# Gate and up as seven block products in place of eight, with the multiplication of activation and up rows left on GpSimd

## The reference

```python
def conv_ffn(h, prev, w_gate, w_up, conv_w, conv_b, w_down):
    g = h @ w_gate
    u = h @ w_up
    l = g.shape[1]
    gp = jnp.concatenate([prev.astype(g.dtype), g], axis=1)
    gc = conv_b
    for i in range(CONV_W):
        gc = gc + conv_w[i] * gp[:, i:i + l]
    y = (jax.nn.gelu(gc) * u) @ w_down
    return y, gp[:, -(CONV_W - 1):]
```

## Time and profile before

| | |
|---|---|
| median of 3 runs | 1596.8 us (1596.42 to 1599.4) |
| profiled execution, device time | 1597.14 us |
| its span in the trace | 1595.6 us |
| mean granted TensorE clock | 0.996 |
| TensorE busy | 1571.7 us (99%) |
| VectorE busy | 783.5 us (49%) |
| ScalarE busy | 565.6 us (35%) |
| GpSimd busy | 387.9 us (24%) |

### The profile page before, as it was taken

How to read it: one execution, slowest core, us unless ns; L and a number is a source line. 1 busy time by engine, 2 the same in 40 slices (tenths; PEclk the granted TensorE clock), 3 DMA queues, 4 the chain that set the end, 5 groups by cost and what they waited for, 6 DMA issues and landing times.

```text
span 1595.6 us, 27497 instructions
## 1 busy us (share of the span) xinstructions
PE 1571.7 (99%) x10810; PEld 1497.5 (94%) x10810; DVE 783.5 (49%) x1022; ACT 565.6 (35%) x888; POOL 387.9 (24%) x421
## 2 busy tenths in 40 slices
PE   9999989999999999999999999999999999999998
PEld 6899879999999999999988997799999999999997
DVE  3324786665543245553322248857554522555522
ACT  4332266245552123322222323643455411333312
POOL 3370020432221012222306402115222200221223
PEclk9999999999999999999999999999999999999998
DMA  5321253222322223322233213612233232232222
GB/s 199 123 76 54 93 186 140 77 99 96 129 97 92 86 90 109 105 67 77 71 102 123 86 47 135 231 59 72 94 130 105 86 102 89 94 129 79 65 73 92
DMA packets 44415, 161.99 MB, mean 102 GB/s; under 512 B 5793, under 2 KB 8257, under 8 KB 43265
## 3 DMA queue, kind: packets, MB, share of 16 engines
q1 hardware_dynamic: 39680, 129.70, 25.0%
q0 software_dynamic: 2464, 28.26, 4.4%
q10 hardware_dynamic: 2208, 3.15, 0.5%
HBM read 149.08 MB, written 30.88 MB: 113 GB/s over the span
## 4 chain that ended last, share of the span: by engine, by line
PE 89%; DVE 6%; ACT 2%; issue 2%; POOL 1%; POOLq 0%; DVEq 0%; ACTq 0%
PE PSUM L1490 62%; PE PSUM L1540 13%; PE PSUM L1565 6%; PE PSUM L1466 4%; PE PSUM L1780 1%; DVE RS L987 1%; PE PSUM L1718 1%; PE PSUM L1556 0%; PE PSUM L1713 0%; DVE SM L1195 0%; ACT WH L728 0%; ACT PS L799 0%; POOL YT L691 0%; DVE XNL L1357 0%; DVE CT L1392 0%
## 5 line engine op out<-in xcount | busy, mean ns | idle before, releaser
L982 DVE TENSOR_TENSOR WL<-RAW,WH 128x1024 fp32r<-128x1024 f32 (+1 forms) x216 | 294.4, 1364 | 489.1 <-ACT WH L728 488.6
L728 ACT ACTIVATE WH<-RAW 128x1024 fp32r<-128x1024 f32 (+1 forms) x216 | 211.9, 982 | 553.9 <-PE PSUM L1490 385.9
L1490 PE MATMUL PSUM<-XFH,WH 128*128 128x320 f32 x1056 | 240.9, 310 | 1.8 <-DVE WL L982 1.2
L1490 PE MATMUL PSUM<-XFH,WL 128*128 128x320 f32 x1056 | 240.0, 309 | 0.0
L1490 PE MATMUL PSUM<-XFL,WH 128*128 128x320 f32 x1056 | 240.0, 309 | 0.0
L1490 PE MATMUL PSUM<-XNH,WH 128*128 128x320 f32 x864 | 198.2, 310 | 1.0 <-DVE XNL L1357 1.0
L1490 PE MATMUL PSUM<-XNL,WH 128*128 128x320 f32 x864 | 196.8, 309 | 0.0
L1490 PE MATMUL PSUM<-XNH,WL 128*128 128x320 f32 x864 | 196.7, 309 | 0.0
L1490 PEld LDWEIGHTS PSUM<-XFH,WH 128*128 128x128 f32 x1056 | 176.2, 188 | 3.0 <-issue 2.7
L1490 PEld LDWEIGHTS PSUM<-XFL,WH 128*128 128x128 f32 x1056 | 176.3, 188 | 0.0
L1490 PEld LDWEIGHTS PSUM<-XFH,WL 128*128 128x128 f32 x1056 | 176.2, 188 | 0.0
(11 more groups left out here) (230 smaller groups left out, 2341.5 us busy)
## 6 DMA issues: line engine op xcount, KB each, us to landing
RAW<-w_gu SPq DMA_DIRECT2D x88, 512.0 KB, 3.5
RAW<-w_in SPq DMA_DIRECT2D x40, 512.0 KB, 3.6
RAW<-w_down SPq DMA_DIRECT2D x32, 384.0 KB, 3.0
RAW<-w_down SPq DMA_DIRECT2D x32, 320.0 KB, 2.7
CAK<-ca_kt SPq DMA_DIRECT2D x16, 512.0 KB, 4.6
CAV<-ca_v SPq DMA_DIRECT2D x16, 512.0 KB, 5.1
RAW<-w_out SPq DMA_DIRECT2D x16, 512.0 KB, 3.6
ca_kt_copy<-ca_kt POOLq DMA_DIRECT2D x16, 512.0 KB, 4.9
```

The costliest lines, as they stand in the source:

```text
L728: nc.scalar.activation(WH[:, s, 0:width], RAW[:, s, 0:width], ACT.Copy).then_inc(hi_ready[s], 1)
L982: nc.vector.tensor_tensor(WL[:, s, 0:width], RAW[:, s, 0:width], WH[:, s, 0:width].bitcast(F32), ALU.subtract).then_inc(lo_ready[s], 1)
L1490: last = nc.tensor.matmul(PSUM[:, b + a, 0:HALF], w[:, s, P * k:P * (k + 1)], x[:, HALF * a:HALF * (a + 1)], start=start and k == 0 and w ...
```

## The change

From tile 3 (PLAIN) on, gate and up of a tile are taken as one product of 2 x 2 blocks. The rows are up (a11, a12) and gate (a21, a22), the inner blocks are the first and the last four of the eight tiles of D_MODEL, and the columns are the two halves of the frames (b11, b12, b21, b22). Seven products of sums of blocks give all four results, in place of eight: a11 b11, s2 t2, s1 t1, s3 t3, a12 b21, a22 t4, s4 b22. Each has 4 x 3 matmuls of 320 columns and a PSUM bank of its own.

- Frames are scaled by gain and RS ahead of the product (`scale_frames`, into XN), and t1 to t4 are formed; all seven are rounded and get a remainder, once a layer, while tiles 0 to 2 run in the old way.
- For each tile, VectorE forms s1 to s4 (512 columns), ScalarE rounds the seven blocks, VectorE takes the seven remainders. WH and WL hold four of them, EXH and EXL three. Loads alternate between RAW and RAW2.
- ScalarE copies a11 b11 into RS, which is free for it now; VectorE adds the products up (`take_...`) into RS, U3, GP and UT.
- Convolution, gelu, YH and YL of a tile move into the next tile's turn on VectorE and ScalarE. Loops over tiles are written out.
- GpSimd's program is the same: it multiplies UT and CT as before.

The diff, cut to its core:

```diff
+PLAIN = 3
+DOWN_UNIT = FFN_UNIT + 2 * PLAIN
+UNITS = DOWN_UNIT + 2 * KT * FFN_HALVES
 SLOT_USES = UNITS // 2
+QUARTER = KT // 2 * P
+PRODUCTS = ("a11", "s2", "s1", "s3", "a12", "a22", "s4")
+MOVING = {"a11": "b11", "s2": "t2", "s1": "t1", "s3": "t3", "a12": "b21", "a22": "t4", "s4": "b22"}
+BLOCK_SUMS = ("s1", "s2", "s3", "s4")
+FRAME_STEPS = tuple(range(KT)) + ("t1", "t3", "t2", "t4")
+FRAME_PARTS = ("b11", "t1", "t2", "t3", "b21", "t4", "b22")
...
+                def block_round(t, name):
+
+                    if name[0] == "a":
+                        act.wait_ge(quarters_loaded[t % 2], quarters_count(l, t))
+                    else:
+                        act.wait_ge(sum_done, sum_count(l, t, name))
+                    if t in (PLAIN, FF_HALF) and PRODUCTS.index(name) < 4:
+                        n = (FFN_UNIT, PLAIN - 1) if t == PLAIN else (DOWN_UNIT, KT - 1)
+                        product_wait(act, l, n[0] + PRODUCTS.index(name) // 2, n[1])
+                    elif folded_index(l, t):
+                        act.wait_ge(block_used, block_count(l, t, name) - len(PRODUCTS))
+                    nc.scalar.activation(block_slot(name)[0], block_source(t, name), ACT.Copy).then_inc(block_hi, 1)
...
+                def y_round(t):
+                    if t == FF_HALF:
+                        product_wait(act, l, DOWN_UNIT + 1, KT - 1)
+                    act.wait_ge(product_done, CREDIT + 2 * (l * FF_TILES + t) + 2)
+                    nc.scalar.activation(YH[:, t % FF_HALF, :], YT[:, :], ACT.Copy).then_inc(y_hi, 1)
...
+                def take_first(t):
+
+                    act.wait_ge(block_used, block_count(l, t, "a11"))
+                    act.wait_ge(folded, 4 * folded_index(l, t))
+                    if t == PLAIN:
+                        act.wait_ge(up_copied, CREDIT + l * FF_TILES + t)
+                    nc.scalar.activation(RS[:, 0:HALF], block_bank("a11"), ACT.Copy).then_inc(first_taken, 1)
...
-                        nc.scalar.activation(YH[:, f, :], YT[:, :], ACT.Copy).then_inc(y_hi, 1)
+                    for t in range(FF_HALF if h else PLAIN + 1, FF_HALF * (h + 1)):
+                        last, inner = t == FF_HALF * (h + 1) - 1, t != FF_HALF
+                        block_round(t, "s4")
+                        take_first(t)
+                        if not last:
+                            block_round(t + 1, "a11")
+                        if inner:
+                            gelu(t - 1)
+                        if last:
+                            down_round(0, h, 0)
+                        else:
+                            block_round(t + 1, "s2")
+                        if inner:
+                            y_round(t - 1)
+                        if last:
+                            down_round(1, h, 0)
+                        else:
+                            block_round(t + 1, "s1")
+                            block_round(t + 1, "s3")
+                        if not last:
+                            block_round(t + 1, "a12")
+                            block_round(t + 1, "a22")
+                        tap(t)
+                    gelu(FF_HALF * (h + 1) - 1)
+                    y_round(FF_HALF * (h + 1) - 1)
...
+                def block_sum(t, name):
+
+                    a = {"s1": ("a21", "a22", ALU.add), "s2": ("s1", "a11", ALU.subtract),
+                         "s3": ("a11", "a21", ALU.subtract), "s4": ("a12", "s2", ALU.subtract)}[name]
+                    dve.wait_ge(quarters_loaded[t % 2], quarters_count(l, t))
+                    if name in ("s2", "s4"):
+                        dve.wait_ge(sum_done, sum_count(l, t, name) - (1 if name == "s2" else 2))
+                    used = {"s1": (t - 1, "s3"), "s2": (t - 1, "s4"), "s3": (t, "s1"), "s4": (t, "s2")}[name]
+                    if folded_index(l, used[0]) >= 0 and used[0] >= PLAIN:
+                        dve.wait_ge(block_lo, block_count(l, *used))
+                    nc.vector.tensor_tensor(block_source(t, name), block_source(t, a[0]), block_source(t, a[1]), a[2])\
+                        .then_inc(sum_done, 1)
+
+                def block_rest(t, name):
+
+                    dve.wait_ge(block_hi, block_count(l, t, name))
+                    high, low = block_slot(name)
+                    nc.vector.tensor_tensor(low, block_source(t, name), high.bitcast(F32), ALU.subtract)\
+                        .then_inc(block_lo, 1)
...
+                def scale_frames(k):
+
+                    nc.vector.scalar_tensor_tensor(out=XN[:, k, :], in0=X[:, k, :],
+                                                   scalar=GAIN[:, bass.ds(l, 1), 1, k], in1=RS[:, :],
+                                                   op0=ALU.mult, op1=ALU.mult).then_inc(frame_step, 1)
...
+                def take_second(t):
+
+                    i = folded_index(l, t)
+                    dve.wait_ge(block_used, block_count(l, t, "s2"))
+                    dve.wait_ge(first_taken, i + 1)
+                    dve.wait_ge(up_copied, CREDIT + l * FF_TILES + t)
+                    nc.vector.tensor_tensor(RS[:, HALF:], block_bank("s2"), RS[:, 0:HALF], ALU.add).then_inc(folded, 1)
+
+                def take_third(t):
+
+                    i = folded_index(l, t)
+                    dve.wait_ge(block_used, block_count(l, t, "s3"))
+                    dve.wait_ge(gate_copied, CREDIT + 2 * (l * FF_TILES + t))
+                    dve.wait_ge(folded, 4 * i + 1)
+                    nc.vector.tensor_tensor(U3[:, :], block_bank("s3"), RS[:, HALF:], ALU.add).then_inc(folded, 1)
+
+                def take_gate_second(t):
+
+                    gate_free(t)
+                    dve.wait_ge(folded, 4 * folded_index(l, t) + 2)
+                    nc.vector.tensor_tensor(streams[:, 1, :, 2:], streams_of(block_bank("s1")[:, 0:HALF_SAMPLE]),
+                                            streams_of(U3[:, 0:HALF_SAMPLE]), ALU.add)
+                    nc.vector.tensor_tensor(GP[:, 2 + HALF_PROMPT:CONV_ROW], block_bank("s1")[:, HALF_SAMPLE:],
+                                            U3[:, HALF_SAMPLE:], ALU.add).then_inc(gate_copied, 1)
+                    nc.vector.tensor_tensor(RS[:, HALF:], block_bank("s1"), RS[:, HALF:], ALU.add).then_inc(folded, 1)
+
+                def take_up_first(t):
+
+                    dve.wait_ge(block_used, block_count(l, t, "a12"))
+                    dve.wait_ge(product_done, CREDIT + 2 * (l * FF_TILES + t))
+                    nc.vector.tensor_tensor(UT[:, 0:HALF], block_bank("a12"), RS[:, 0:HALF], ALU.add).then_inc(folded, 1)
+
+                def take_gate_first(t):
+
+                    dve.wait_ge(block_used, block_count(l, t, "a22"))
+                    nc.vector.tensor_tensor(streams[:, 0, :, 2:], streams_of(block_bank("a22")[:, HALF_PROMPT:]),
+                                            streams_of(U3[:, HALF_PROMPT:]), ALU.add)
+                    nc.vector.tensor_tensor(GP[:, 2:2 + HALF_PROMPT], block_bank("a22")[:, 0:HALF_PROMPT],
+                                            U3[:, 0:HALF_PROMPT], ALU.add).then_inc(gate_copied, 1)
+
+                def take_up_second(t):
+
+                    dve.wait_ge(block_used, block_count(l, t, "s4"))
+                    dve.wait_ge(folded, 4 * folded_index(l, t) + 3)
+                    nc.vector.tensor_tensor(UT[:, HALF:], block_bank("s4"), RS[:, HALF:], ALU.add)\
+                        .then_inc(up_copied, 1)
...
+                rstd_ready.wait(dve, l, "ffn")
+                dve.wait_ge(pads_zeroed, l + 1)
+                lo(l, FFN_UNIT + 2, 0)
+                take_gate(0)
+                for k in range(4):
+                    scale_frames(k)
+                convolve(0)
+                for k in range(4, KT):
+                    scale_frames(k)
+                take_up(0)
+                lo(l, FFN_UNIT + 3, 0)
+                frame_sum("t1")
+                y_rest(0)
+                frame_rest("b11")
+                lo(l, FFN_UNIT + 2, 1)
...
+                    for t in range(FF_HALF if h else PLAIN + 1, FF_HALF * (h + 1)):
+                        last, inner = t == FF_HALF * (h + 1) - 1, t != FF_HALF
+                        if inner:
+                            take_up_second(t - 1)
+                            convolve(t - 1)
+                        block_rest(t, "s4")
+                        if not last:
+                            block_sum(t + 1, "s1")
+                            block_sum(t + 1, "s2")
+                        take_second(t)
+                        if last:
+                            down_rest(0, h, 0)
+                        else:
+                            block_rest(t + 1, "a11")
+                            block_rest(t + 1, "s2")
+                            block_rest(t + 1, "s1")
+                            block_sum(t + 1, "s3")
+                        take_third(t)
+                        take_gate_second(t)
+                        if inner:
```

(72 more changed lines are left out.)

293 lines of the change are left out of this document (221 added, 72 removed).

## The result

| | before | after |
|---|---|---|
| median of 4 runs each, the same chip | 1597.13 us (1596.42 to 1599.40) | 1616.49 us (1616.32 to 1616.73) |
| span of the profiled execution | 1595.6 us | 1614.7 us |
| mean granted TensorE clock | 0.996 | 0.986 |

The changed kernel takes 1.012 times as long (95% interval 1.0108 to 1.0132): 19.4 us more. The forecast was +36 us, 1633 in a range of 1590 to 1662. The sign, the range and the mechanism held; the size was 17 us too large.

The account below looks back on a forecast made before the run. TensorE's matmuls bound the kernel before; VectorE would bind after, at 14.4 us a folded tile against 12.32. Halves at +17.0 and +1.0 us, over two layers, add 36 to 1597.1: 1633 us, range 1590 to 1662.

Parts of the forecast that it names:

- The tile: Steady folded tile: VectorE needs 14.4 us, against TensorE's 12.32 and 14.08 before the change.
- back-to-back work: VectorE's 23 instructions over 9,824 columns in a folded tile, one behind the other: 12.0 us.
- waits for the direct neighbour: Four times in a folded tile a VectorE instruction waits for the one right ahead: 0.22 us each, together 0.9.
- GpSimd's multiplication holds a sum: In each folded tile GpSimd's multiplication falls on VectorE's sums for the next tile and holds them up: 0.9 us.
- convolution waits for the tap: In each folded tile convolution on VectorE waits for ScalarE's tap after the last copy into GP: 0.2 us.
- round of s1 late behind YH: ScalarE rounds s2, then YH, and only then s1, so VectorE waits 0.4 us in each folded tile.
- the rival of 1660: Every GpSimd instruction, small copies included, is paid in full by VectorE: 15.3 us a tile, 1660 us; chance 0.15.
- VectorE binds, but the waits close: GpSimd's turn falls on additions out of PSUM, ScalarE never late: 12.9 us a tile, 1588 us; chance 0.15.
- The way in: VectorE's work before its first steady tile: 55.8 us, plus 3.3 for GpSimd's multiplications and some 4 of waits, ending at 404.3.
- The end of a half: Last tile of a half, with no next tile to prepare: its chain through convolution, gelu, multiplication and YH reaches YL at 17.5 us.
- Tile 11: Second half's first tile, prepared while down runs: its own iteration is paced by nothing but VectorE, 14.3 us.
- The wait before down: Down's second product waits several us for YL; new waits before down, some 4 then 3 us, could lower the clock.

Follow-up runs that it names:

- Experiment 1: Changed kernel with GpSimd multiplying only 8 of 512 prompt columns and one of each 16 sample columns: 1582.45 us, ratio 0.9908 to the kernel before.
- experiment 2: Changed kernel with GpSimd multiplying 256 of 512 prompt columns and all sample columns: 1595.66 us, ratio 0.9987 to the kernel before.
- experiment 5: Changed kernel with VectorE's addition at L1655 (into RS) cut to 8 of 320 columns: 1605.94 us, ratio 1.0042 to the kernel before.
- experiment 4: Changed kernel with the additions out of PSUM moved ahead of s2's sum, and ScalarE rounding YH ahead of s2: 1586.60 us, ratio 0.9930 to the kernel before.
- experiment 7: Experiment 4's order, with s4's remainder between the convolution steps and y's remainder between s1's remainder and s3's sum: 1604.78 us, ratio 1.0036 to the kernel before.
- experiment 6: Changed kernel with the remainders of t1 to t4 on the way in taken over 2 of 320 columns of each block: 1609.39 us, ratio 1.0064.
- 9: Experiment 4's order, with s4's remainder between the convolution steps except in each half's last iteration: 1582.58 us, ratio 0.9908 to the kernel before.

## Why the prediction was right in sign and too high in size

**The mechanism** held in its main parts: VectorE became the bound of the folded tile, TensorE waits for WL (31.0 us; for EXL no wait shows), L782 stands ahead of a stretched sum, and VectorE waits for the round of s1. Experiments 1, 2 and 5 change VectorE's time in three ways, and the tile follows each of them.

**The tile, 14.4 forecast, 13.95 measured**, by its terms:

| term | forecast | measured |
|---|---|---|
| back-to-back work | 12.0 | 12.0 |
| waits for the direct neighbour | 0.9 | 0.7 |
| GpSimd's multiplication holds a sum | 0.9 | 0.92 |
| convolution waits for the tap | 0.2 | 0.07 |
| round of s1 late behind YH | 0.4 | 0.24 |

The first is what is left of 13.95 after the others. The tile's 23 records, with s2's sum at 0.69, bear it out: they add up to 13.78 us, less 23 x 0.08 is 11.9. The four pairs show gaps of 0.04, 0.10, 0.11 and 0.14 us after the record's end; with 0.08 of lost overlap each, 0.71. The forecast took the one pair that the trace of before shows, the convolution steps with 0.14, for all four; in the changed kernel that very pair shows 0.04. The last term does not depend on when L782 starts or ends: ScalarE begins its round of s2 when s2's sum ends, and YH and the round of s1 follow without a wait. The round of s1 ends 1.81 us after the sum (609.45 to 611.26), where the forecast had 2.0; VectorE gets there in 1.60, as forecast. Experiment 1 agrees: the sum is 0.91 us shorter there, and the wait is 0.20.

**GpSimd's turns.** The small copies did not cost VectorE anything measurable: s2's sum is its only instruction that is stretched in the steady tiles. GpSimd is the one that waits (L787 0.89 us in place of 0.43, TAIL's first copy 0.48 in place of 0.19). That is against the rival of 1660. The Trainium skill, "SBUF — State Buffer", section "Who interferes with whom", says that VectorE instructions with at most one SBUF input, outside its 2-port modes, do not contend with GpSimd, and that whoever issues first holds the shared pair of ports; the trace agrees on both: additions at 0.49 beside L782 in experiment 4, s2's sum at 1.60 when L782 came first, L787 at 0.89 when the sum did. The forecast's own evidence for additions out of PSUM, that L1399 and L1385 show no stretch, was none: no multiplication runs beside them in its rows (L1399 ends at 620.80, L686 starts at 620.88). Experiment 4 is what shows it.

**The rival "VectorE binds, but the waits close"** asked that GpSimd's turn fall on additions out of PSUM and that ScalarE be never late, and gave 1588. That was not this kernel, but experiment 4 is it: 13.00 us a tile and 1586.6. Its point of decision, 13.2 us a tile, is about where the runs put it: 13.00 is faster, 13.44 (experiment 7), 13.64 and 13.95 are slower, and 13.42 came out level, with a shorter way in and shorter ends (experiment 2).

**The way in, 63.4 forecast, 62.9 measured.** (Where it starts in layer 0 differs, 339.5 to 341.4 us among the profiles of this study, and was not traced.) The sum of VectorE's work, with the waits added, was right to 1%; experiment 6 shows that VectorE sets it for the most part.

**The end of a half, 17.5 forecast, 16.4 measured** (486.07 to 502.51). Gate's first half is in GP after 9.3 us, against 9.7; the rest of the chain is shorter by 0.7.

**Tile 11, 14.3 forecast, 15.3 measured.** It was said to be paced by VectorE alone. It has two waits for ScalarE's rounds, right behind down's last addition:

```profile
575.02 0.49 DVE L1805 TENSOR_TENSOR X<-PSUM,X 128x320 f32<-128x320 f32 x1 [1.71 <-PE PSUM L1845]
575.75 0.69 DVE L1572 TENSOR_TENSOR WL<-SUM,WH 128x512 fp32r<-128x512 f32 x1 [0.23 <-ACT WH L1026]
...
577.94 0.69 DVE L1572 TENSOR_TENSOR WL<-SUM,WH 128x512 fp32r<-128x512 f32 x1 [0.70 <-ACT WH L1026]
...
590.28 0.48 DVE L1675 TENSOR_TENSOR UT<-PSUM,RS 128x320 f32<-128x320 f32 x1
```

**The wait before down** stands in another place than forecast. Down's second product was to wait several us for YL; in the first half it waits 0.36. The first product waits 4.04 us, for take_up_first (L1661), which empties a bank. The time lost is nearly the same, since YL at 502.51 comes nearly as late as said. The clock behind that wait (below) adds 0.5 us in the second half and 0.9 in the third; the forecast had it in the range as a few us.

**The sum.** Against the forecast: thirty steady tiles at -0.45 (13.5 us), four ends at -1.1 (4.4), two ways in at -0.5 (1.0), less two tiles 11 at +1.0 and the clock's 1.4: 15.5 us, and 36 - 20.2 = 15.8 is what the two feed-forward parts came out below it. (The other 1.1 us between the 20.2 and the span's 19.1 lies outside of them.) The step that failed is a size: the waits on VectorE inside the steady tile were taken 0.45 us too long, 0.2 of it in the waits for the direct neighbour (0.9 against 0.7), the rest in the waits for the tap and for the round of s1.

**Where the gain of the seventh product went.** 66.9 us less of matmuls are there. TensorE's tile of 12.32 us now waits for one of 13.95, and the way in and the ends of halves have grown to what VectorE and the chain behind it need. Experiments 4 and 9 got back 34 us by order alone; the work of VectorE that is left, 12.0 us back to back, is close under TensorE's 12.32.

## What to carry to other kernels

When work moves to an idle engine until it is nearly as full as the one it relieves, the order of its instructions decides the sign: the same work gave 1.2% slower and 0.9% faster here. Put the instructions with one input in PSUM beside the other engine's multiplication, and know of each instruction which round on a third engine it covers before you move it (0.70 us a tile in experiment 7). A saving in the steady tile must be followed to the loop's last iteration, where nothing is left to hide a chain that has become later.

## What the runs showed of the hardware that was not expected

A wait of a VectorE instruction for the one right ahead of it is not one price: in the changed kernel the gap is 0.04 us between the convolution steps and 0.10 to 0.14 us between the other pairs, against 0.08 us of overlap without a wait. Nor is it the price of a pair: the same two convolution steps have 0.14 to 0.16 us in all 44 tiles of the kernel before, and 0.04 in all 44 of the changed one. Its loop over tiles is written out now; whether that is the cause was not tried. Putting another instruction between the convolution steps gave back 0.10 us a tile (13.00 to 12.90). The Trainium skill, "VectorE: DVE Perf Modes", section "The DRAIN you can't avoid", has eight copies take the same time with a semaphore after each as with one at the end. Here raising a semaphore shows no cost either: L1572 and L1565 each raise one, and where the next instruction does not wait for it, it still starts 0.08 us ahead of their end. It is the wait for the neighbour's semaphore that costs, 0.12 to 0.22 us.

Behind the 4 us without a matmul ahead of down, TensorE's granted clock falls below its upper level. Windows behind three of the four halves (us, then busy times as above, then clock; behind the fourth, from 1521 to 1529, it is 0.79):

```profile
495.00:502.50 7.50, 6.88 (x36) 6.62 (x36) 3.36 (x6) 2.63 (x4) 3.63 (x7) 0.78 0.30 85
725.00:733.00 8.00, 7.94 (x38) 7.95 (x39) 3.13 (x5) 2.42 (x3) 2.54 (x5) 0.66 0.21 66
1291.00:1299.00 8.00, 8.00 (x36) 8.00 (x37) 2.98 (x4) 2.42 (x3) 3.68 (x7) 0.62 0.35 109
```

0.78, 0.66 and 0.62 are means of the two levels, 1.2 and 2.4 GHz: down's first matmuls are 0.27 us apart, until 498.5 in the first window and until 730.5 in the second, and 0.147 after that. In the first the second product still waits for YL, and the clock costs nothing. In the second the second product starts only at 732.84, behind the 36 matmuls of the first and 0.6 us after YL is there (in the third 0.9; in the first, with nothing else to wait for, 0.05): the wait for VectorE is paid a second time, in clock.
